# Three ways between the stages of a transformer's first block: column sums of 128 columns, and transposes by token tile

## The reference, cut to what matters

```
cond = silu(c)
for i in range(2):
    mod = cond @ ada_w[i] + ada_b[i]
    sh1, sc1, g1, sh2, sc2, g2 = split(mod, 6)
    h = rms_norm(x, norm_mix[i]) * (1.0 + sc1) + sh1
    x = x + g1 * mixer_i(h)            # i = 0: attention, i = 1: spatial gating
    h = rms_norm(x, norm_ffn[i]) * (1.0 + sc2) + sh2
    x = x + g2 * (square(relu(h @ ffn_w1[i])) @ ffn_w2[i])
x = second_block(x)
```

## Time and profile before

| What | us |
|---|---|
| median of 3 runs | 1061.75 |
| lowest and highest | 1059.44 and 1065.32 |
| span of the profiled execution | 1059.8 |
| TensorE busy in it | 1026.2 |
| VectorE busy in it | 765.8 |
| ScalarE busy in it | 550.5 |
| way 1, first filler to first product of the next stage | 176.25 to 188.10 |
| way 2 | 371.86 to 382.36 |
| way 3 | 597.62 to 606.71 |

### The profile page before, as it was taken

One profiled execution on the slowest core, in us unless ns is written; L12 is line 12 of the kernel. 1 busy time (PEld: TensorE's weight loads), 2 busy tenths in 40 slices (PEclk: granted clock), 3 DMA queues, 4 the chain that ended last, 5 costly groups with the idle time before them and its releaser, 6 DMA issues.

```text
span 1059.8 us, 17084 instructions
## 1 busy us (share of the span) xinstructions
PE 1026.2 (97%) x6050; PEld 899.0 (85%) x6050; DVE 765.8 (72%) x1368; ACT 550.5 (52%) x918; POOL 101.4 (10%) x160
## 2 busy tenths in 40 slices
PE   6999989999999999999999999999999999899996
PEld 6887878899999988889999899999988888788885
DVE  5788787987888677777768755655568786587863
ACT  1457755534544456644344435444346676566662
POOL 0041101000000010011000000000004021030210
PEclk9699999899999989999999999999999999999998
DMA  9966755688787638857686464566427540175501
GB/s 370 334 228 215 256 190 208 217 291 299 266 276 275 232 129 311 284 211 240 217 275 209 156 189 158 191 202 201 168 100 239 193 163 23 60 264 183 169 11 41
DMA packets 57197, 218.46 MB, mean 206 GB/s; under 512 B 6420, under 2 KB 11540, under 8 KB 51000
## 3 DMA queue, kind: packets, MB, share of 16 engines
q1 hardware_dynamic: 48368, 169.24, 46.6%
q0 software_dynamic: 6048, 43.52, 11.4%
q10 hardware_dynamic: 2728, 5.00, 1.5%
HBM read 216.67 MB, written 1.06 MB: 205 GB/s over the span
## 4 chain that ended last, share of the span: by engine, by line
PE 88%; DVE 4%; ACT 3%; DMA 2%; issue 1%; POOL 0%; SPq 0%; ACTq 0%; DVEq 0%
PE ps L1743 26%; PE ps L1744 25%; PE ps L1745 25%; PE ps L1847 2%; PE ps L2225 2%; PE ps L1812 1%; PE ps L1802 1%; PE ps L1792 1%; DVE w_lo L1008 1%; PE ps L2115 1%; PE ps L2273 1%; DMA arena<-in_adastream 1%; PE ps L1835 1%; ACT w_hi L554 1%; DMA raw<-in_wstream 1%
## 5 line engine op out<-in xcount | busy, mean ns | idle before, releaser
L1008 DVE TENSOR_TENSOR w_lo<-raw,w_hi 128x1024 fp32r<-128x1024 f32 (+1 forms) x312 | 355.5, 1180 | 64.5 <-ACT w_hi L554 57.7
L554 ACT ACTIVATE w_hi<-raw 128x1024 fp32r<-128x1024 f32 (+1 forms) x312 | 307.1, 1020 | 134.4 <-DMA raw<-in_wstream 96.2
L1743 PE MATMUL ps<-h_hi,w_hi 128*128 128x256 f32 x704 | 201.8, 287 | 1.0 <-DVE h_lo L1087 0.8
L1744 PE MATMUL ps<-h_lo,w_hi 128*128 128x256 f32 x704 | 200.4, 285 | 0.0
L1745 PE MATMUL ps<-h_hi,w_lo 128*128 128x256 f32 x704 | 200.3, 285 | 0.0
L1743 PE MATMUL ps<-w_hi,h_hi 128*128 128x512 f32 (+1 forms) x480 | 190.4, 397 | 4.7 <-DVE h_lo L1087 3.0
L1745 PE MATMUL ps<-w_hi,h_lo 128*128 128x512 f32 (+1 forms) x480 | 184.5, 384 | 0.0
L1744 PE MATMUL ps<-w_lo,h_hi 128*128 128x512 f32 (+1 forms) x480 | 184.5, 384 | 0.0
L1743 PEld LDWEIGHTS ps<-h_hi,w_hi 128*128 128x128 f32 x704 | 136.3, 194 | 4.1 <-issue 2.6
L1743 PE MATMUL ps<-w_hi,a_hi 128*128 128x512 f32 x352 | 137.4, 390 | 1.5 <-DVE a_lo L1461 1.5
L1744 PE MATMUL ps<-w_lo,a_hi 128*128 128x512 f32 x352 | 137.2, 390 | 0.0
(11 more groups left out here) (221 smaller groups left out, 1331.1 us busy)
## 6 DMA issues: line engine op xcount, KB each, us to landing
raw<-in_wstream SPq DMA_DIRECT2D x296, 512.0 KB, 5.2
ada_raw<-in_adastream POOLq DMA_DIRECT2D x40, 1024.0 KB, 5.1
ada_raw<-in_adastream SPq DMA_DIRECT2D x4, 1024.0 KB, 9.3
arena<-in_adastream SPq DMA_DIRECT2D x4, 1024.0 KB, 10.7
row<-in_gate_rows ACTq DMA_DIRECT2D x5, 512.0 KB, 4.1
raw<-in_wsmall SPq DMA_DIRECT2D x16, 128.0 KB, 2.2
row<-in_params POOLq DMA_DIRECT2D x2, 769.0 KB, 5.3
x<-in_x SPq DMA_DIRECT2D x1, 1024.0 KB, 9.6
```

Of the source, the lines that this page charges most:

```text
L554: act.activation(w_hi[:, c % SPLIT, at], raw[:, n, 0:width // 2], ACT.Copy)\
L1008: nc.vector.tensor_tensor(w_lo[:, c % SPLIT, at], raw[:, (2 * c + h) % RAW, 0:width // 2], w_hi[:, c % SPLIT, at].bitcast(F32), ALU.subtract)\
L1743: nc.tensor.matmul(dst, sh, mh, start=start, stop=False)
L1744: nc.tensor.matmul(dst, sh, ml, start=False, stop=False)
```

## The change

`columns` gets a width. On the three ways it multiplies with all 128 columns of `ones`, each sum thus standing in 128 equal columns of the bank, and the next one starts a column further on, so that columns 0 to 15 hold the 16 sums as before. The fillers between the sums are gone. A new function `transition` holds the way: the sums, the transposes of tile 0, three fillers, the transposes of tile 1 (which alone wait for the second `norm_x`), three fillers. On DVE `norm_x` of tile 0 stands ahead of `modulation` and that of tile 1 behind it. The first way of all, at the kernel's start, stays with one column.

```
-            def norm_x(base, turn=0):
-                for t in range(TT):
-                    dve.wait_ge(s_rinv, turn + (base + t + 1))
+            def norm_x(base, tokens=range(TT)):
+                for t in tokens:
+                    dve.wait_ge(s_rinv, base + t + 1)
...
-            norm_x(2)
+            norm_x(2, (0,))
             modulation(1, 0)
+            norm_x(2, (1,))
...
-            def transpose_x(n):
-                for t in range(TT):
+            def transpose_x(n, tokens=range(TT)):
+                for t in tokens:
                     pe.wait_ge(s_xn, 2 * n + t + 1)
...
-            def columns(a0, bank, outs=range(16), filled=()):
+            def columns(a0, bank, outs=range(16), width=1):
 
                 for b in outs:
-                    if b in filled:
-                        keep_warm_wide(7, 1)
                     a = (a0 + b // 2 + ADA_AT) % ADA_KEPT
-                    last = nc.tensor.matmul(ps[:, bank, b:b + 1],
+                    last = nc.tensor.matmul(ps[:, bank, b:b + width],
                                             ada_acc[:, a, (b % 2) * P:(b % 2 + 1) * P],
-                                            ones[:, 0:1], start=True, stop=True)
+                                            ones[:, 0:width], start=True, stop=True)
                 last.then_inc(s_modps, 1)
+
+            def transition(n, a0):
+
+                pe.wait_ge(s_res, 2 * n - 1)
+                columns(a0, 0, width=P)
+                transpose_x(n, (0,))
+                keep_warm_wide(2, 3)
+                transpose_x(n, (1,))
+                keep_warm_wide(2, 3)
...
             pe.wait_ge(s_gate, 2)
             pe.wait_ge(s_ada, 20)
-            pe.wait_ge(s_res, 1)
-            columns(12, 0, filled=range(0, 16, 2))
+            transition(1, 12)
...
-            transpose_x(1)
             mlp_stage(0, 0, 8, 20)
...
-            pe.wait_ge(s_res, 3)
-            columns(24, 0, filled=range(0, 16, 4))
-            transpose_x(2)
+            transition(2, 24)
...
-            pe.wait_ge(s_res, 5)
-            columns(36, 0, filled=range(0, 16, 2))
-            transpose_x(3)
+            transition(3, 36)
```

More of the change, by code:

```diff
@@ L1412, in mlp_stage @@
                     lo_part(c0 + 34, 0, CW)
-                    norm_x(4)
+                    norm_x(4, (0,))
                     modulation(2, 0)
+                    norm_x(4, (1,))
                     lo_part(c0 + 34, 1, CW)
@@ L1471, in _ @@
             lo_part(C_GU + 26, 0, CW)
-            norm_x(6)
+            norm_x(6, (0,))
             modulation(3, 0)
+            norm_x(6, (1,))
             lo_part(C_GU + 26, 1, CW)
```

## The result

The changed kernel takes 1053.37 us, the median of 9 runs (1052.40 to 1057.23), against 1059.44 us of the kernel before in 9 runs beside it (1055.80 to 1065.32). The ratio is 0.9936 with a 95% interval of 0.9913 to 0.9958, so 0.64% or 6.8 us are won. A second timing on another occasion gave 0.9942 (0.9921 to 0.9964). The medians' difference is 6.1 us in the first and 5.1 us in the second; the ratio weighs the runs better, as single executions of either kernel spread over 5 to 13 us.

A forecast was written before the change was run, and what follows sets the result against it. TensorE, busy 1026.2 of 1059.8 us, was taken to bound the kernel, losing time to half clock on the ways. Gains of 5.18, 2.20 and 0.79 us sum to 8.17; 1061.75 - 8.2 gave 1053.5 us, range 1049 to 1059.

The forecast's parts named there:

- The ways' full-clock times: Way 1 at full clock: sums 3.76 us, ACT starting at 182.21 us, first product at 184.56 instead of 188.10.
- way 1 to way 2: Way 1 and the stage behind it, up to the first `down` chunk, at full clock: 5.18 us won.
- way 3 to the end: Way 3, already at full clock before: ACT starts at 603.57 instead of 604.36 us, 0.79 us won.
- way 2 to way 3: Way 2 at full clock: first product at 380.16 instead of 382.36 us, 2.20 us won, nothing behind it.
- Split into clock and shorter ways: Over the three ways, 8.17 us won in sum, of which 4.40 and some 2.3 are clock.
- the new order of sums and transposes alone: On the ways, it would bring 0.8 us on ways 1 and 3 and lose 0.1 on way 2.
- the 1.95 us between span and median: Whole kernel before: the median lies 1.95 us above the profile's span, let stand as nothing showed its origin.
- The clock fell: Rival: TensorE's clock still falls on a way, giving back 4.4 or 2.3 us; 1055.8 to 1057.9 us, chance 0.15.
- transposes hold or raise the clock: On way 2 before, the clock rose at about 381.7 us after only transposes and a wait; argued against further falls.
- The gain was not eaten behind way 1: Rival: PE waits for `a_lo` behind way 1, which gives 2.96 us in place of 5.18; 1055.7 us, chance 0.12.
- The sums were not dear: Rival: wide sums on the ways cost 0.236 us a record, 7.55 us in all; 1064.6 us, chance 0.05.
- Slower: Rival: the new way as a whole runs at half clock, sums taking 7.3 us; 1073 us, chance 0.04.

The follow-up runs named there:

- the doubled ones: The changed kernel with every wide sum made twice, 64 records instead of 32 on each way; 1062.58 us, ratio 1.0014 to the kernel before.
- the order alone: The changed kernel with the old one-column sums and their old fillers, its order of transposes, norms and modulation kept; 1063.14 us, ratio 1.0023 to the kernel before.
- the second profile of before: The kernel before, with no edit, profiled again and timed against itself; 1062.28 us, ratio 1.0025.
- thin sums, new order: The changed kernel with its sums back at one column and no fillers among them; 1057.97 us, ratio 0.9976 to the kernel before.

## Why the prediction was right, and where it was off

*The ways' full-clock times.* By the steps of the prediction ACT would start 5.96 us after the start of way 1 and the first product come at 8.31; measured are 6.06 and 8.41, the same on all ways. The sums cost 3.57 us (the doubled ones measure it) where 3.76 was taken; tile 0 starts 3.95 us in against 3.89. The 0.1 us is in the second tile's start (5.58 against 5.51) and in ACT's. The second norm kept its place, with the modulation ahead of it.

*The terms.* Between the profiles, way 1 to way 2 gave 5.1 us (forecast 5.18), way 3 to the end 0.8 (0.79), way 2 to way 3 3.0 (2.20). Of the last, 2.1 are the way itself; 0.8 more were a wait of PE for `a_lo` in the spatial gating that is 1.5 us in the first profile of before and 0.7 in the second, 0.6 in that of the changed kernel. Why it was longer in that one execution isn't settled.

*Split into clock and shorter ways.* The forecast put 6.7 of 8.2 us on the clock and 1.5 on the shorter ways. The second is 876.2 - 874.7 = 1.5 us, as forecast. But the forecast calls this the gain of "the new order of sums and transposes alone", and that is not what the runs show: the order alone gained nothing, and wide sums without fillers made the ways as short in the old order. The first is the step that was mis-sized: it took the falls of the profiled execution for those of every execution and took the whole gain off the median. Three profiles lost 7.4, 1.0 and 4.8 us, 4.4 on average, and 4.4 + 1.5 = 5.9 us is near the 6.2 and 6.8 that the two ratios give. Of the 1.95 us between span and median that the forecast left unexplained, some 1.7 is what every run's time has over its span. That the forecast time of 1053.5 came within 0.2 us of 1053.37 is partly luck: the median of before went from 1061.75 in 3 runs to 1059.44 in 9, which made up for a gain sized 1.4 us too high by the ratio and 2.1 by the medians. The second timing gave 1055.77, as more of its runs had the late start.

*The rivals.* The clock fell on none of the six ways of the two profiles of the changed kernel. That transposes hold or raise the clock was read from way 2 before; the run without fillers neither proves nor refutes it, because its falls come behind both transposes and 2 us of near idleness. The Trainium skill's rule that transposes do not count as busy in the same way ("TensorE: Matmul & The Clock Gate", Part 4: PE-mode transpose) would fit those falls, but not the rise at 381.7 with nothing but transposes and a wait ahead of it. Way 3 in the second profile of before shows it once more, with no wait:

```profile
595.88 3.55 PE L1793 MATMUL ps<-ident,arena 128*128 128x128 f32 x16
```

The clock fell at 595.8, PE took nothing but these 16 transposes, and the clock was at 1.00 again from 599.2 on (the 0.60 of the window above is 3.2 us of half clock in 4). So for the float32 transposes of this kernel the traces speak against the rule twice. Whether they run in the mode that the page means isn't told by the profile, which lists them as MATMUL, and no run was made to test the rule. The gain was not eaten behind way 1: `a_lo` keeps 0.9 us of cover where 0.6 was forecast. The sums were not dear: 0.112 us a record. Slower did not happen with the changed kernel, but one half of it alone, the order, is no gain at all (1.0023).

*What remains open.* How often the clock falls on the ways of the changed kernel: none in two profiles (6 of 9 ways in before) does not say never. The mean clocks of the runs say more, if runs with the same start are compared (last section): 0.986 to 0.989 in eleven runs and 0.993 to 0.997 in nine, against 0.973 to 0.985 in 52 and 0.983 to 0.995 in 45 runs of the kernel before. So no run of the changed kernel lost as much clock as the usual run of before. The spread of its runs, 1052.4 to 1058.4, comes mostly from the start. Which of the six fillers is needed is open too; that some are of use is suggested by the four falls on the 9 ways without any behind the sums.

## What to carry to other kernels

Where PE waits on a chain of other engines anyway, make its small matmuls wider instead of putting fillers among them: here 128 columns cost what one column costs, the result is the same, and on none of 24 ways did the clock fall among them. Move a wait for PE ahead of a critical instruction only when PE's part surely ends before that instruction is due; here DVE still waits 0.37 us for POOL behind the modulation, and with late sums the order lost 0.56 us on way 2 (8.86 against 8.30). Before a gain is counted on from falls of the clock in one profile, take two or three more of the same kernel: the falls move, and one execution had seven times the loss of another.

## What the runs showed of the hardware that was not expected

*128 columns cost what one costs.* From the first to the last of the 32 records it is 3.38 us with one column and 3.46 with 128, both at full clock.

*Wide sums let the clock stand where thin ones do not.* PE is busy without a gap during both, but 11 of 15 ways with one-column sums have a fall on or right behind them and none of 24 with 128 columns.

*The stage ahead of way 1 varies by almost as much as the change brings.* Identical instructions took 175.8 to 176.5 us in six profiles (the early start) and 179.0 to 181.8 in the other seven (the late start). In the first profile of before, an early one, 64 one-column records, the first matmul of the first projection and the first one at full clock stand so:

```profile
20.78 11.53 PE L1847 MATMUL ps<-cond,arena 128*128 128x1 f32 x64
...
40.03 0.80 PE L1743 MATMUL ps<-w_hi,h_hi 128*128 128x512 f32 x1
...
43.93 0.39 PE L1743 MATMUL ps<-w_hi,h_hi 128*128 128x512 f32 x1
```

In that of the changed kernel, a late one:

```profile
21.35 13.81 PE L1857 MATMUL ps<-cond,arena 128*128 128x1 f32 x64
...
42.88 0.80 PE L1746 MATMUL ps<-w_hi,h_hi 128*128 128x512 f32 x1
...
48.45 0.40 PE L1747 MATMUL ps<-w_lo,h_hi 128*128 128x512 f32 x1
```

The 64 records take 2.28 us longer and the projection begins 2.85 us later. Its 128x512 records are then 0.43 us apart until 48.2 us, in the early start only until 43.8, and 0.23 apart afterwards; that costs the other 0.8 of the 3.6 us between the two starts. In the early start the clock is on record as 1.00 between 20.0 and 23.3 us and 0.50 from there to 43.8. In the late start it reads 1.00 up to 48.2 us as well, but 0.43 us is the spacing of the half clock, so the record misses this stretch. What decides between the two starts isn't known.

This is why the mean clocks of executions can't be compared as they stand: 0.997 here for a run of 1056.26 us, and 0.986 to 0.989 for runs of 1052.4 to 1054.4. They can be compared among runs with the same start. All runs come apart into two groups by span and mean clock together, as the 13 profiles do; for a run without a profile of its own this is inferred from the two numbers.

| Kernel | early start: runs, median span, clock | late start: runs, median span, clock |
|---|---|---|
| before | 52, 1057.5, 0.973-0.985 | 45, 1062.1, 0.983-0.995 |
| changed | 11, 1051.4, 0.986-0.989 | 9, 1055.2, 0.993-0.997 |
| thin sums, new order | 8, 1055.7, 0.976-0.982 | 4, 1060.4, 0.986-0.991 |

The change brings 6.1 us in the one group and 6.9 in the other, and of the 6.1 the width of the sums alone, in the new order, brings 4.3 (1055.7 to 1051.4).
